# Hybrid trunk with experts: the work between two couples of experts laid out over the column chunks, and a seventh weight slot

## What is computed

```python
def swiglu(x, w1, w3, w2):
    return (jax.nn.silu(x @ w1) * (x @ w3)) @ w2

def moe_ffn(xn, router_w, router_b, w1, w3, w2):
    logits = (xn @ router_w).astype(jnp.float32) + router_b.astype(jnp.float32)
    top_v, top_i = lax.top_k(logits, TOP_K)
    w = jax.nn.softmax(top_v, axis=-1)
    gate = jnp.sum(jax.nn.one_hot(top_i, N_EXPERTS, dtype=jnp.float32) * w[..., None], axis=-2)
    ...
    for e in range(N_EXPERTS):
        out = out + gate[..., e:e + 1] * swiglu(xn, w1[e], w3[e], w2[e])
    return out
```

## Time and profile before

| | us |
|---|---|
| median of three runs | 1785.7 (1784.58 to 1787.78) |
| the profiled execution | 1791.94 |
| its span | 1790.0 |
| TensorE busy | 1694.1 (95%) |
| VectorE busy | 1090.3 (61%) |
| ScalarE busy | 886.0 (49%) |
| moved from memory | 483 MB, 271 GB/s over the span |

### The profile page before, as it was taken

The page is one execution under the profiler, slowest core; times in us unless marked ns, Lnnn a source line. Parts: engine busy times, 40 slices in busy tenths (PEclk is TensorE's granted clock), DMA queues, the critical chain, the costliest instruction groups (busy, mean ns, idle before and its releaser), DMA issues. The chain is left out here.

```text
span 1790.0 us, 27179 instructions
## 1 busy us (share of the span) xinstructions
PE 1694.1 (95%) x10162; PEld 1302.1 (73%) x10163; DVE 1090.3 (61%) x1690; ACT 886.0 (49%) x1339; POOL 19.9 (1%) x51
## 2 busy tenths in 40 slices
PE   7899899999999999897999999999999999999988
PEld 5788899999997888896565665656655556656557
DVE  7696876665677796865464545555446454455536
ACT  6577544433355678434454544444434454444434
POOL 3000000000000000000000000000000000000000
PEclk9999999999999999998999999999999999999999
DMA  8333362644543433433999978999879999699961
GB/s 312 142 123 126 136 224 109 253 158 158 220 147 135 146 150 106 165 137 132 377 420 420 421 321 349 420 420 421 361 317 418 416 419 402 275 418 422 420 280 66
DMA packets 61883, 485.98 MB, mean 271 GB/s; under 512 B 6832, under 2 KB 9152, under 8 KB 10944
## 3 DMA queue, kind: packets, MB, share of 16 engines
q1 hardware_dynamic: 61584, 484.09, 67.5%
q10 hardware_dynamic: 176, 0.15, 0.1%
HBM read 483.15 MB, written 1.07 MB: 271 GB/s over the span
## 5 line engine op out<-in xcount | busy, mean ns | idle before, releaser
L2054 DVE TENSOR_TENSOR w_lo<-raw,w_hi 128x1024 fp32r<-128x1024 f32 x336 | 396.1, 1222 | 241.2 <-ACT w_hi L957 234.4
L957 ACT ACTIVATE w_hi<-raw 128x1024 fp32r<-128x1024 f32 x336 | 336.3, 1050 | 183.9 <-DMA raw<-in_moe_w 183.3
L476 DVE TENSOR_TENSOR w_lo<-raw,w_hi 128x1024 fp32r<-128x1024 f32 x236 | 283.4, 1220 | 111.9 <-ACT w_hi L471 111.0
L1109 PE MATMUL work<-x_r,w_hi 128*128 128x256 f32 x1024 | 299.5, 293 | 15.4 <-DVE w_lo L476 11.5
L1110 PE MATMUL work<-x_r,w_hi 128*128 128x256 f32 x1024 | 291.8, 285 | 0.0
L1111 PE MATMUL work<-x_r,w_lo 128*128 128x256 f32 x1024 | 291.4, 285 | 0.0
L471 ACT ACTIVATE w_hi<-raw 128x1024 fp32r<-128x1024 f32 x236 | 241.1, 1048 | 68.9 <-PE work L1111 29.7
L1109 PEld LDWEIGHTS work<-x_r,w_hi 128*128 128x128 f32 x1024 | 198.4, 194 | 24.7 <-issue 18.6
L1109 PE MATMUL work<-w_hi,bias_r 128*128 128x512 f32 x448 | 185.9, 415 | 25.1 <-DVE w_lo L2054 17.8
L1441 PE MATMUL acc<-raw,bias 128*64 128x512 f32 x896 | 204.6, 598 | 0.0
L1110 PEld LDWEIGHTS work<-x_r,w_hi 128*128 128x128 f32 x1024 | 198.6, 194 | 1.0 <-issue 0.8
(11 more groups left out here) (340 smaller groups left out, 2596.9 us busy)
## 6 DMA issues: line engine op xcount, KB each, us to landing
raw<-in_moe_w SPq DMA_DIRECT2D x336, 1024.0 KB, 10.0
raw<-in_mix_w SPq DMA_DIRECT2D x33, 2048.0 KB, 7.8
raw<-in_dense_w SPq DMA_DIRECT2D x21, 2048.0 KB, 8.0
raw<-in_ple_w SPq DMA_DIRECT2D x4, 2048.0 KB, 10.0
raw<-in_mix_w SPq DMA_DIRECT2D x4, 512.0 KB, 7.1
areaK<-in_ple_p SPq DMA_DIRECT2D x2, 1024.0 KB, 9.6
hT<-in_xT SPq DMA_DIRECT2D x4, 256.0 KB, 6.1
gate_b<-bias_line SPq DMA_DIRECT2D x1, 1024.0 KB, 5.8
```

The source lines that it names most:

```text
L476: eng.tensor_tensor(unit(w_lo, g), raw_part(g), unit(w_hi, g).bitcast(F32), ALU.subtract).then_inc(split_ok, 1)
L957: act.activation(w_hi[n % UNITS_HELD][:, :], heavy_quarter(where, j), ACT.Copy).then_inc(m_hi_ok, 1)
L1109: pe.matmul(out, stat[0], move[0], start=start, stop=False, skip_group_check=True)
L2054: dve.tensor_tensor(w_lo[u][:, :], heavy_quarter(where, n % HEAVY_C), w_hi[u][:, :].bitcast(F32), ALU.subtract).then_inc(m_split, 1)
```

## The change

The work that is done once a couple is spread: a new `between(i, c)` puts one piece between the two up products of each chunk. Chunks 0 to 3 have one row of the combine each, chunk 4 the gather of the next couple's light tokens, chunks 5 and 6 one half each of the next heavy tokens' gather. The gates are transposed in chunk 4. All pieces use the bank misc; the gates use pv_ps. Gathered tokens are copied to a spare area (areaB: `stage`, `stage_light`) by ScalarE and go from there to xg_hi, xg_lo and xg_light when the couple before is done with those. VectorE's splits 6 and 7 now stand ahead of the one addition per chunk; its tables are built after chunk 1 (picks) and chunk 5 (gates). The first couple's light gather is made before the loop, and VectorE copies it. A seventh slot of 1 MiB lies in x1, half t of chunk c is in slot (12c + t) % 7, and a load waits for the half that came seven before it.

```diff
-SLOTS = 2 * RING
+RAW_SLOTS = 2 * RING
+SLOTS = RAW_SLOTS + 1
+        stage = areaB[:, 0:1024].rearrange("p (k n) -> p k n", k=KT)
+        stage_light = areaB[:, 1024:1536].rearrange("p (k n) -> p k n", k=KT)
         def half_slot(s):
+            if s == RAW_SLOTS:
+                return x1[:, 0:HALF]
             return raw[s // 2][:, (s % 2) * HALF:(s % 2 + 1) * HALF]
+        def slot_of(where, c, t):
+            return t if where == "extra" else (HALVES_C * c + t) % SLOTS
...
             def load_couple(heavy, light, i, c, t, to):
+                gone, old = divmod(HALVES_C * c + t - SLOTS, HALVES_C)
+                if old < 4:
+                    ge(sp, m_split, "couple", i, HEAVY_Q, HEAVY_Q, HEAVY_C * gone + 2 * (old + 1))
+                elif old < 8:
+                    ge(sp, l_used, "couple", i, LIGHT_N, 0, LIGHT_C * gone + old // 6 + 2)
+                elif old < 10:
+                    ge(sp, m_split, "couple", i, HEAVY_Q, HEAVY_Q, HEAVY_C * gone + 2 * (old - 3))
                 else:
-                    ge(sp, l_used, "couple", i, LIGHT_N, 0, LIGHT_C * c + 2)
+                    ge(sp, l_used, "couple", i, LIGHT_N, 0, LIGHT_C * gone + old - 6)
...
+            def stage_gathered(i, half):
+                ge(act, m_gathered, "couple", i, 2, 2, half + 3)
+                act.activation(stage[:, 4 * half:4 * half + 4, :], misc[:, :].rearrange("p (k n) -> p k n", k=4),
+                               ACT.Copy).then_inc(m_staged, 1)
+            def next_tokens(i):
+                ge(act, m_used, "couple", i, HEAVY_Q, HEAVY_Q, UNITS_HELD + HEAVY_C * (FC - 1) + 8)
+                ge(act, m_staged, "couple", i, 2, 0, 2)
+                for half in range(2):
+                    k = slice(4 * half, 4 * half + 4)
+                    act.activation(xg_hi[:, k, :], stage[:, k, :], ACT.Copy).then_inc(m_xg_hi, 1)
...
             def turn_light(i, c):
                 ge(pe, l_both_ok, "couple", i, FC, 0, c + 1)
-                if c:
-                    ge(pe, l_hid_ok, "couple", i, FC, 0, c)
+                if c < 4:
+                    ge(pe, m_added, "couple", i, 4, 4, c + 1)
+                elif c == 4:
+                    ge(pe, l_staged, "couple", i, 1, 0, 2)
                 else:
-                    ge(pe, m_gtaken, "couple", i, 1, 1, 2)
+                    ge(pe, m_staged, "couple", i, 2, 0, c - 4)
+            def between(i, c):
+                if c == 0:
+                    ge(pe, l_staged, "couple", i, 1, 0, 1)
+                    ge(pe, m_y, "couple", i, 1, 1, 1)
+                    ge(pe, m_gtaken, "couple", i, 1, 1, 1)
+                if c < 4:
+                    combine_row(misc, c)
+                elif c == 4:
+                    gather_light(i, 1)
+                else:
+                    gather_half(i, c - 5)
             def couple(i):
                 for c in range(FC):
                     up("couple", i, 0, c)
-                    if c == 0:
-                        gather_light(i)
-                        combine("couple", i)
+                    between(i, c)
                     up("couple", i, 1, c)
-                    if c == 0:
+                    if c == 4:
                         turn_gates("couple", i)
                     for k in range(KT):
                         up_light(i, c, k)
                         if k == 1:
                             turn("couple", i, c)
-                    if c == FC - 1:
-                        gather("couple", i, 1)
```

More of the change, by code:

```diff
@@ L411, in trunk @@
         l_xg_ok = sem("l_xg_ok")
+        l_staged = sem("l_staged")
+        m_staged = sem("m_staged")
         m_built = sem("m_built")
@@ L638, in _ @@
                     light = expert_of(slice(1, 2))
-                    for t in range(4, 6):
+                    for t in range(4, SLOTS):
                         load_half(light, t, 0)
@@ L648, in _ @@
                         light = expert_of(bass.ds(i * 2 + 3, 1))
-                        for t in range(6):
+                        for t in range(SLOTS):
                             load_couple(heavy, light, i, FC, t, 0)
@@ L654, in _ @@
                     for c in range(FC):
-                        for t in range(0 if c else 6, HALVES_C):
+                        for t in range(0 if c else SLOTS, HALVES_C):
                             load_couple(heavy, light, i, c, t, c)
@@ L664, in _ @@
                             for c in range(FC):
-                                for t in range(SLOTS):
+                                for t in range(RAW_SLOTS):
                                     load_extra(e, r, c, t)
@@ L971, in take_gates @@
                 ge(act, m_gturned, where, i, 1, 1, 1)
+                turned = misc if where == "extra" else pv_ps
                 if where == "extra":
@@ L1368, in combine @@
                         ge(pe, m_added, where, i, 4, 4, r - 1)
-                    for b in range(2):
-                        out = (pv_ps, misc)[r % 2][:, T * b:T * b + T]
-                        pe.matmul(out, y_sb[:, (4 * b + r) * P:(4 * b + r + 1) * P], m_gpickT,
-                                  start=True, stop=False, skip_group_check=True)
-                        mm = pe.matmul(out, y_light[:, r * P:(r + 1) * P], l_gpickT[b],
-                                       start=False, stop=True, skip_group_check=True)
-                    mm.then_inc(m_combined, 1)
+                    combine_row((pv_ps, misc)[r % 2], r)
             def part(where, i, n):
@@ L1401, in turn @@
                     ge(pe, m_hidT, where, i, FC, FC, c)
-                else:
+                elif where == "extra":
                     ge(pe, m_added, where, i, 4, 4, 3)
+                if c == 4 and where == "couple":
+                    ge(pe, m_gtaken, where, i, 1, 1, 2)
                 for ft in range(FT):
@@ L2037, in build_light, with next_tokens_lo @@
                 ins.then_inc(m_gbuilt, 1)
+            def next_tokens_lo(i):
+                for half in range(2):
+                    ge(dve, m_xg_hi, "couple", i, 2, 2, half + 3)
+                    k = slice(4 * half, 4 * half + 4)
+                    dve.tensor_tensor(xg_lo[:, k, :], stage[:, k, :], xg_hi[:, k, :].bitcast(F32), ALU.subtract).then_inc(m_xg, 1)
             def split_gathered(where, i, more):
@@ L2047, in add_combined @@
                 ge(dve, m_combined, where, i, 4, 4, r + 1)
-                dve.tensor_tensor(added(hT, r), added(hT, r), (pv_ps, misc)[r % 2][:, :].rearrange("p (k t) -> p k t", k=2),
+                sums = misc if where == "couple" else (pv_ps, misc)[r % 2]
+                dve.tensor_tensor(added(hT, r), added(hT, r), sums[:, :].rearrange("p (k t) -> p k t", k=2),
                                   ALU.add).then_inc(m_added, 1)
@@ L2119, in moe @@
                 split_gathered("couple", 0, 0)
+                dve.wait_ge(l_gathered, 1)
+                dve.tensor_copy(stage_light, misc[:, :].rearrange("p (k n) -> p k n", k=KT)).then_inc(l_staged, 1)
                 with dve.Fori(0, COUPLES) as i:
```

170 lines of the change are left out of this document (104 added, 66 removed).

## The result

The kernel with the change takes **1777.95 us** (median of six runs, 1776.93 to 1779.09) beside 1786.51 us for the kernel before (1784.58 to 1790.48): a ratio of 0.9944, interval 0.993 to 0.9959. It is faster by 8.6 us, which the interval tells from no change; 20.1 were forecast. The forecast had the sign, its range held the time, and its main number was 12 us too low. The profiled span went from 1790.0 to 1777.0, by 13.0. That is 4.4 more than the medians say, because the profiled execution of before (1791.94) lies 5.4 above the median of its runs, and that of after (1779.09) only 1.1.

What follows compares the result with a forecast made beforehand. Transfers at 420 GB/s were taken to bind plain chunks, with the queue standing still behind a couple's start. -26.5 (waits) + 3.2 + 2.4 + 0.8 = -20.1 us off the 1785.7 median gave 1765.6; range 1757 to 1785.

Steps and rivals of the forecast that it cites:

- the loop gap: TensorE's gaps of about 3 us where its loop goes round between couples: taken to stay, with their slow products.
- (b): Couple's last chunk: gather no longer covers work on the next tokens; TensorE waits 0.6 us, 2.4 in all (0 to 6).
- A chunk of 28.75: TensorE's own need for a plain chunk without waits, 28.75 us, chosen between 28.63 and 28.86.
- (a): Four more pieces a couple between products of another type, each slowing the product behind by 0.2 us: 3.2 in all.
- (c): Stage entry: VectorE waits for the new light gather and copies it ahead of its first split, costing 0.8 us.
- (d): Added waits for misc, copies of the light tokens and VectorE's pick tables within the chunks: cost nothing.
- Can seven slots feed it: Weight loads through seven slots keep up with 30.5 us chunks; smallest margin 3.8 us, at half 0.
- The slow products: Some 13 products at 0.43 instead of 0.23 us behind each loop gap, 2.6 us each; 2.4 at the entry.
- Half fed: Whatever holds the weight queue leaves short waits of 0.35 us in 28 chunks, 10 us, giving 1776 us; chance 0.17.
- Late landing: Loads landing after 10.0 us even with an empty queue lengthen each of 28 chunks by 1.2: 1800 us; chance 0.07.
- The waits are not the transfers': The 1.1 us a chunk are hand-overs from ScalarE to VectorE to TensorE and stay: +6.4, 1792 us; chance 0.05.
- The loop gap is data: TensorE's gaps between couples are waits for data and go with their slow products: another -9.2 - 7.8, 1749 us; chance 0.06.

Runs made afterwards that it cites:

- kernel 1: The changed kernel with six waits of ScalarE's loop body left out that another wait implies, body 252 instructions instead of 258: 1759.48 us, ratio 0.9843.
- kernel 10: kernel 1 with the next tokens' copies and subtractions moved behind quarters 10 and 11 on ScalarE and VectorE: 1758.54 us, ratio 0.9836.
- kernel 4: The changed kernel with six weight slots instead of seven, ScalarE's loop body 260 instructions: 1783.37 us, ratio 0.9983.
- kernel 9: kernel 1 with six weight slots instead of seven, ScalarE's loop body 254 instructions: 1769.42 us, ratio 0.9901.
- kernel 8: The kernel before with the seventh slot alone and no work moved, ScalarE's loop body 252 instructions: 1774.95 us, ratio 0.9927.
- kernel 3: kernel 1 with TensorE's loop over the four couples written out in the code: 1746.15 us, ratio 0.9769.
- 12: The changed kernel measured again without an edit, ScalarE's loop body 258 instructions: 1778.51 us, ratio 0.9952.

## Why the prediction was right and wrong

**The step that failed is "the loop gap ... I take it as the cost of going round and leave it".** It asked what going round costs TensorE, and left out that ScalarE and VectorE go round as well. ScalarE's turn stood in the trace of before with 0.97 us, and the change adds four instructions to that body. The step put the change of the gaps at nothing; it is +13.2 us, and all of it is on the path. Without the pause (kernel 1) the gain is 28 us. The forecast looked at the change as work to be moved, and costed its operations; the length of a loop body was no item.

Could the rows of before have given the 13? Not the size. The nearest row for a turn that costs is TensorE's, 3 us, and its body is 929 instructions long. VectorE's body has 228 and pauses in neither kernel. Of ScalarE's turn some 5 us were free in before, from the chain of the earlier trace rows: its w_lo was done at 1048.84 and TensorE started at 1053.17, 4.3 later, with a turn of 0.97 ahead. So a price of 3 would have been put down at nothing, and the true one only begins to count above 5. But a rival with a place and a point from which it decides could have been written: a body that has grown, at an engine that is always early, by less than 5 us it is free, from there it is lost three times. The count of instructions was to be had from the program. The rule that the prediction cites for TensorE, in the Trainium skill, "Runtime: NRT & Kernel Launch", section Instruction fetch mechanics, also speaks of each engine, and of instructions that are fetched in blocks of 256. By it a body above the block could have been suspected on ScalarE too. The runs agree with that number (256 free, 258 not), but the page's rule is of a window of two such blocks, and, worked out from its figures, a body of 258 gets beyond two blocks only if it begins with the last instruction of one. All bodies that pause here begin at the same place, so the runs don't tell whether they do so, or whether the window is shorter than the page has it. The page has no price for the fetch, and the runs show 5.2 and 10.5 us.

The other steps, in their order:

- **What bounded the kernel: right.** In the plain chunks the transfers were the bound and are no more: ScalarE's waits 183.3 to 42.3, TensorE's some 55 waits to 8. The 26.5 us of waiting are gone but for what term (b) leaves.
- **A chunk of 28.75: 28.65.** The difference is 2.8 us over 28 chunks.
- **(a) Changes of kind, 3.2: next to nothing.** The 0.2 behind a piece is there, as the rows below show: from 895.98 the second product starts 0.42 later, where 0.23 is usual. But the piece itself, from 894.44 to 895.98, is 1.54 long and not the 1.70 taken from a quarter of the earlier trace rows, for that quarter held such a step already. 1.54 + 0.19 = 1.73.
TensorE's timeline of the kernel after, the piece of chunk 1:

```profile
894.44 0.59 PE L1408 MATMUL misc<-gate_b,spare 128*128 128x256 f32 x2
...
895.98 0.58 PE L1143 MATMUL work<-w_hi,bias_r 128*128 128x512 f32 x1
896.40 0.40 PE L1144 MATMUL work<-w_lo,bias_r 128*128 128x512 f32 x1
896.63 0.39 PE L1145 MATMUL work<-w_hi,bias_r 128*128 128x512 f32 x1
```

- **(b) The last chunk, 0.6 a couple: 0.8.** The wait is there with 0.56 at 1037.31, and kernel 10 removes it.
- **(c) The entry, 0.8: about 0.6.** The stage starts 1.2 later in the profiled execution (826.52 against 825.33). But a product ahead of the stage that is the same in both, `misc<-gate_a`, already starts at 810.97 instead of 810.37; counted from there the entry is 15.55 and 14.96 away. In all fourteen traces the stage starts at 822.5 to 826.5, with either code.
- **(d) Added waits, nothing: right.** None of them appears in the waits list.
- **Can seven slots feed it: right.** DMA share 0.94 to 1.01, no wait at a chunk's first product. The same reckoning, done for six slots in what was expected of kernel 4, gave no waits, and was wrong by 10 us (kernel 9 against 1). So that it came out for seven says little for the reckoning itself.
- **The slow products, left as they were: mis-sized.** The 2.6 a gap was read behind the first gap of before. Counted as the excess over steps of 0.23, they cost 2.9 there and only 1.6 and 1.5 behind the other two, 6.0 and not 7.8, so the waiting in before was 28.3 and not 26.5. In the kernel after they cost 2.4, 2.3 and 2.3, 6.9 in all, 0.9 more. At the entry they cost 1.8 instead of 2.5; in the second measurement of the same kernel it is 2.5 again, behind the same idle time of 2.65, so this 0.7 is not the change's.

The sum with the measured terms: -28.3 (waits), + 3.2 (b), + 13.2 (gaps), - 2.8 (unit), + 0.9 - 0.7 (slow products) = -14.5; the stage shrank by 14.8. With its start 1.2 later that is 13.3 to 13.6, and the span went down by 13.0. Without the gaps the sum is -27.7. Kernel 1's stage is 31.0 below that of before: 27.7, 2.1 by slow products that the kernel after has more, and 0.7 by gaps shorter than before's, make 30.5. So the forecast of 20.1 was wrong twice within the span, in opposite directions: it missed a loss of 13, and was some 6 too careful in small terms ((a), the unit and the slow products, less (b) and the entry). The 7.1 that are left of the two, and the 4.4 by which the profiled execution of before was off its median, are the 11.5 between 20.1 and 8.6. That the range held the time is owed to the two errors covering each other in part.

**The rivals.** Half fed: no; behind a couple's first product no chunk but its last has a wait on TensorE, and the plain ones are 30.34 to 30.41 in every couple. Late landing: no; the median landing is 10.2 to 10.6, above the 8.8 from which it was to decide, and it costs nothing, since a half that takes long stands behind others and not behind an idle queue. The waits are not the transfers': no, kernel 8 moves no work and wins 13 with a slot. The loop gap is data: no, kernel 3.

**Where the gain is.** The slot alone gives 13.5 us (kernel 8), the spreading alone 18.6 (kernel 9), both 28.3 (kernel 1), less than the sum of 32.1, which fits that they cover in part the same waits. The pause takes 14 to 19 of it (kernel 9 against 4, kernel 1 against 12), and 8.6 to 9.6 is left.

## What to carry to other kernels

Count the instructions of each engine's loop body before and after an edit, waits and register operations too: here a body of 256 was free and one of 258 at the same place cost ScalarE 10.5 us each time round, and six waits that another wait implied, taken out, were worth more than the change itself. An engine that is far from the bound has a deadline all the same where a loop turns; work out how long it may stand there (6 us here) and look at its row for "issue". Where a gap at a turn names data, write out that one engine's loop: if the gap goes, it was the turn.

## What the runs showed of the hardware

- ScalarE's turn of a loop shows no pause with 252, 254 or 256 instructions in the body, and one of 10.4 to 11.1 us with 258 (10 with 260), in two kernels, the body beginning at the same place in all of them. A body of 254 that began 32 instructions later had none either. The label is "issue", and the instruction queue has some five packets of 8 KB more for each turn, three of them inside the pause.
- With little else in the queues (84 GB/s) the same turn costs 5.2 to 5.6 us. How the rest comes about, whether the packets queue behind weights or are only slowed by them, was not measured.
- TensorE's turn costs some 3 us with a body of 919 to 929 instructions (2.6 to 3.3 in the kernels without ScalarE's pause), far less than ScalarE's with 258, and nothing where the loop is written out. Why is open.
- After a gap of 7.6 us TensorE's granted clock was 0.60 over the 10 us around it, that is time at 1.2 beside time at 2.4 GHz, and ten of its steps were about 0.43 before it returned to 0.23; with no gap (kernel 3) there were none. What the slow steps cost does not follow the length of the gap: 1.5 us behind 7.07 and 3.0 behind 6.88 in kernel 4, 2.9 behind 2.97 and 1.6 behind 2.91 in before, 0.1 behind 2.75 in kernel 8.
